# Attention over eight pairs of heads: five device loops, and the same passes written out

## The reference

```python
for blk in range(S // Q_BLOCK):
    q0 = blk * Q_BLOCK
    q1 = q0 + Q_BLOCK
    s = jnp.einsum("bhqd,bhkd->bhqk", q[:, :, q0:q1], k[:, :, :q1]).astype(jnp.float32)
    s = s + cum[:, :, q0:q1, None] - cum[:, :, None, :q1]
    causal = (q0 + jnp.arange(Q_BLOCK))[:, None] >= jnp.arange(q1)[None, :]
    p = jax.nn.softmax(jnp.where(causal, s, -jnp.inf), axis=-1)
    outs.append(jnp.einsum("bhqk,bhkd->bhqd", p.astype(v.dtype), v[:, :, :q1]))
```

## Time and profile before

| what | value |
| --- | --- |
| median of 3 runs | 2577.97 us |
| lowest and highest run | 2575.59 and 2579.7 us |
| the profiled execution | 2578.18 us |
| its span, first to last instruction | 2576.3 us |
| mean granted TensorE clock | 0.970 |
| PE busy in the span | 2410.6 us, 94% |
| DVE, ACT, POOL busy | 1350.7, 1160.1, 623.2 us |
| instructions executed | 41772 |
| instruction fetches, q8 and q14 | 59 packets, 0.97 MB, and 70 packets, 0.57 MB |

### The profile page before, as it was taken

How to read it: one execution, slowest core, us unless ns; L and a number is a source line. 1 busy time by engine, 2 the same in 40 slices (tenths; PEclk the granted TensorE clock), 3 DMA queues, 4 the chain that set the end, 5 groups by cost and what they waited for, 6 DMA issues and landing times. The chain is left out here.

```text
span 2576.3 us, 41772 instructions
## 1 busy us (share of the span) xinstructions
PE 2410.6 (94%) x13921; PEld 2081.1 (81%) x13921; DVE 1350.7 (52%) x2840; ACT 1160.1 (45%) x2136; POOL 623.2 (24%) x740
## 2 busy tenths in 40 slices
PE   8899999999996999999999999699689999993998
PEld 7688889998885888888888888587578888872786
DVE  4312121211007888888888888543245666575343
ACT  4211111111115888888888888510034555565100
POOL 0000000000002555455554555334300000000254
PEclk9899999999998999999999999899889999997999
DMA  5434343332116444544455444366344354343653
GB/s 183 113 113 126 113 130 114 124 106 78 65 49 148 98 98 111 128 113 98 96 124 129 99 98 96 106 215 212 125 154 123 123 156 138 117 146 120 246 189 138
DMA packets 216353, 325.75 MB, mean 126 GB/s; under 512 B 16672, under 2 KB 141664, under 8 KB 210016
## 3 DMA queue, kind: packets, MB, share of 16 engines
q1 hardware_dynamic: 215712, 323.68, 43.9%
q0 software_dynamic: 512, 0.53, 0.1%
HBM read 197.79 MB, written 126.35 MB: 126 GB/s over the span
## 5 line engine op out<-in xcount | busy, mean ns | idle before, releaser
L760 DVE TENSOR_TENSOR at_pl<-at_tps,at_ph 128x512 fp32r<-128x512 f32 (+3 forms) x640 | 370.5, 603 | 22.3 <-ACT at_ph L705 22.1
L705 ACT ACTIVATE at_ph<-at_tps 128x512 fp32r<-128x512 f32 (+3 forms) x640 | 313.0, 529 | 105.7 <-PE at_tps L627 98.9
L323 ACT ACTIVATE pa_stg<-pa_ps 128x512 fp32r<-128x512 f32 (+1 forms) x128 | 76.4, 599 | 608.4 <-PE pa_ps L227 608.3
L627 PE MATMUL at_tps<-at_ident,at_probs 128*128 128x128 f32 x2176 | 337.8, 273 | 1.5 <-DVE at_pl L760 1.2
L642 PE MATMUL at_ops<-at_ph,at_val 128*128 128x256 f32 (+1 forms) x1152 | 325.3, 304 | 2.3 <-DVE at_pl L760 2.1
L227 PE MATMUL pa_ps<-pa_xh,pa_wh 128*128 128x512 f32 x800 | 313.1, 391 | 12.1 <-DVE pa_stg L390 9.6
L695 ACT ACTIVATE at_probs<-at_probs,at_least 128x128 f32<-128x128 f32 (+15 forms) x256 | 307.7, 1202 | 19.0 <-DVE at_probs L751 18.9
L227 PE MATMUL pa_ps<-pa_xl,pa_wh 128*128 128x512 f32 x800 | 312.4, 390 | 0.0
L227 PE MATMUL pa_ps<-pa_xh,pa_wl 128*128 128x512 f32 x800 | 312.3, 390 | 0.0
L612 PE MATMUL at_sps<-at_k,at_q 128*128 128x512 f32 (+3 forms) x640 | 271.5, 424 | 26.4 <-DMA at_k<-forget_sums 22.0
L642 PE MATMUL at_ops<-at_pl,at_val 128*128 128x256 f32 (+1 forms) x1152 | 294.9, 281 | 0.0
(11 more groups left out here) (165 smaller groups left out, 4669.8 us busy)
## 6 DMA issues: line engine op xcount, KB each, us to landing
at_q<-q_halves SPq DMA_DIRECT2D x48, 512.0 KB
at_k<-k_halves SPq DMA_DIRECT2D x48, 512.0 KB
pa_wst<-in_attn_w_in SPq DMA_DIRECT2D x16, 1024.0 KB, 7.3
q_halves<-pa_stg SPq DMA_DIRECT2D x32, 512.0 KB, 3.7
k_halves<-pa_stg SPq DMA_DIRECT2D x32, 512.0 KB, 3.7
v_halves<-pa_stg SPq DMA_DIRECT2D x32, 512.0 KB, 2.8
at_val<-v_halves SPq DMA_DIRECT2D x16, 1024.0 KB, 16.9
y_gated<-rep_work SPq DMA_DIRECT2D x32, 512.0 KB, 2.9
```

The source lines that it names most:

```text
L323: nc.scalar.activation(out, source(kind, s), func, scale=scale).then_inc(evac_h, 1)
L627: mm = nc.tensor.transpose(tps[c % TB][:, k, :], probs[s % ROWS][:, t0:t0 + P], ident[:, :])
L705: nc.scalar.activation(ph[g % 2][:, j * PB:j * PB + n, i % 2 * P:(i % 2 + 1) * P], tps[c % TB][:, 0:n, :], ACT.Copy).then_inc(high_out, 1)
L760: nc.vector.tensor_tensor(pl[g % 2][at], tps[c % TB][:, 0:n, :], raw(ph[g % 2][at]), ALU.subtract)\
```

## The change

In each of the five blocks of `attend` the device loop becomes a Python loop over the same range. The body is then put down seven times (six on SP) with `it` as a plain number. The order of the work, all tiles and all waits stay.

```diff
@@ sync
             pair(0, False)
-            with sp.Fori(1, PAIRS - 1) as it:
+            for it in range(1, PAIRS - 1):
                 pair(it, False)
@@ gpsimd
             pair(0)
-            with pool.Fori(1, PAIRS) as it:
+            for it in range(1, PAIRS):
                 pair(it)
@@ tensor
-            with pe.Fori(1, PAIRS) as it:
+            for it in range(1, PAIRS):
                 for s in range(STEPS):
                     step(it, s, True)
@@ scalar
-            with act.Fori(1, PAIRS) as it:
+            for it in range(1, PAIRS):
                 for s in range(STEPS):
                     step(it, s, True)
@@ vector
-            with dve.Fori(1, PAIRS) as it:
+            for it in range(1, PAIRS):
                 for s in range(STEPS):
                     step(it, s, True)
```

## The result

The changed kernel takes 2580.94 us (median of 22 runs, 2577.55 to 2583.02), the kernel before in the same runs 2576.56 us (22 runs, 2572.98 to 2580.24). The ratio is 1.0016 with a 95% interval of 1.0009 to 1.0022: slower by 2 to 6 us. The ratio is just inside the 0.2% that the prediction called no change; the upper end of the interval is just outside. It had forecast 2579.1 us, with 2574.5 to 2584.0 as its range.

What follows compares the result with a forecast made beforehand. The prediction took PE to bound attention, with DVE not far behind. Its terms, -0.4 + 0 + 0 + 1.5 = +1.1 us on the profiled execution (2578.18 us, 0.2 above the median), gave 2579.1 us, range 2574.5 to 2584.

Steps and rivals of the forecast that it cites:

- 1. back edges: Attention's loop: six taken back edges go, which together cost PE 0.4 us; term -0.4 us.
- 2. register instructions: Attention's loop: register instructions go, at most 34 us on PE, but sequencers run ahead and hide them; term 0.
- 3. fetching PE's code: Attention: every pass of PE's code is now fetched, some 36 packets more; bounds 0 and 21.7 us, taken as 0.
- 4. the late L751: DVE in attention: pair 0's 0.36 us delay may recur in written-out pairs; bounds 0 and 3.1 us, term +1.5 us.
- more or less often than in half of the pairs: Sign on DVE in attention: term 4 is wrong if single late L751 come at such a rate.
- A: Rival: DVE's stall at attention's back edges counts in full, 18.6 us gained, giving 2559.6; chance 5%.
- B: Rival: register instructions were on PE's path in attention, 34 us gained, giving 2544; chance 2%.
- C: Rival: fetching PE's code stalls once in each pair, 21.7 us lost, giving 2600; chance 9%, smaller forms included.
- D's upper end: Case within the forecast (81% with D): DVE's odd 0.36 us comes in every attention pair, giving 2580.9.

Runs made afterwards that it cites:

- e2: The kernel before with DVE alone written out, the other engines keeping their loops: 846.4 us in attention, first to last L648.
- e1: The changed kernel with the loop put back on DVE alone: 841.8 us in attention, first to last L648.
- e3: The changed kernel with one more instruction on DVE ahead of attention: 842.4 us in attention, ratio 1.0009 to the kernel before.
- e4: The changed kernel with sixteen more instructions on DVE ahead of attention: 845.3 us in attention.
- e5: e3 with DVE's wait for PE's scores named before the wait for the transposes, so a row's first L751 carries the former: 840.0 us in attention.
- e9: e5 with, in later chunks, L751 carrying the wait for DVE's own minimum and the scores' wait alone: 836.0 us in attention; 2571.44 us, ratio 0.9983 to kernel before.
- e6: e5 with the same exchange of waits on ACT: 840.2 us in attention, ratio 0.9995 to the kernel before.
- e10: The kernel before, loops kept, with e9's order of waits on DVE: 842.6 us in attention, ratio 1.0002 to the kernel before.

## Why the prediction was right

The forecast, a little slower and hardly more than a measurement can tell, held, and its range held the median. As a difference it was too small: the measured 2 to 6 us lie wholly above its +1.1. It also owes something to luck, since two parts that it put at nothing, -1.0 and +2.2 us, partly cancel. Attention's 3.1 us come out of its terms like this:

| part | forecast | measured |
| --- | --- | --- |
| 1. back edges | -0.4 | -0.5: what the six passes of the kernel before, up to 106.04 us, have over 105.73 |
| 2. register instructions | 0 | -1.0: 7 x (105.73 - 105.59), the other engines' loops; -1.1 by e2 against the changed kernel; DVE's own 0 |
| 3. fetching PE's code | 0 | 0: e1 |
| 4. the late L751 | +1.5 | +2.5: 7 x 0.36, e3 and e4 |
| which wait stands alone | not seen | +2.2: 7 x (105.88 - 105.56), e3 against e5 |

The sum of what was measured is 2.5 + 2.2 - 0.5 - 1.0 = 3.2. Each part is from one profile, and the first is the least certain: DVE's six edges in e1 cost 1.3 us against e5 (634.7 us for the six passes, and 633.4).

Term 4 was the step with the wrong size. The prediction had found the event and its length in the earlier trace rows and left open what it was: "a packet of instructions ending there" or chance. It took half of the bound, since one of two fresh passes had it. The first was the cause as far as the count goes, and the event came in all seven pairs; by the prediction's own sign ("more or less often than in half of the pairs") the term is wrong. That attention's loss equals the upper bound of 3.1 us is partly chance, since terms 1 and 2 and the order of waits are in it too. What could have been done blind: to count DVE's instructions in the written order of the changed kernel up to that L751 and go on in steps of 128. That count gave seven exposed places in pairs 1 to 7 for this kernel, none for one instruction more and seven for sixteen more, before e3 and e4 ran.

Term 2 read "no gain" from pair 0's 77.87 us against 77.43. But pair 0 has the late L751 and the early wait carried, and under these two losses the gain can't be seen. e1 shows it: its pairs take 77.34 us for the same eleven groups. What the term also passed over is that register instructions carried waits. The prediction said that "waits on numbers remain in the instructions, or stand alone as before"; which of two waits stands alone changed, and this costs 0.09 us at each first L751 of a row where the scores come late.

The rivals. A, the whole DVE stall of 18.6 us: refuted, six edges on DVE are worth 1.3 us (e1 against e5, which both let L751 carry the late wait). B, 34 us of register instructions: refuted by e1 and e2, which leave about 1 us. C, PE's code late: refuted by e1 and by e9, whose pairs are all at 105.07 us with the whole code fetched. D's upper end is what happened. The stalls behind DVE's branches did go, and seven ends of a block came into the open. The Trainium skill, "Runtime: NRT & Kernel Launch", section "Instruction fetch mechanics", calls the crossing of a block mostly hidden, and on DVE the trace agrees for most of them: of 19 in pairs 1 to 7, twelve don't show.

What stays open: by its ratio the changed kernel loses 4.1 us and in attention 3.1. The other written-out kernels with 11 runs lean the same way: e3 has +2.3 us and in attention +0.2, e6 -1.3 and -2.0, e9 -4.4 and -6.2, while e10, with loops, has +0.5 and +0.4. This could be 1 to 2 us outside attention that go with longer code, but each interval is about 2 us wide on either side, and no stage of the profiles shows it.

## What to carry to other kernels

Before a loop is written out, compare a pass of it with the same work where it is already straight, and look at what differs: here that showed the late L751 before anything ran, while the 3 us stall behind a branch looked like the prize and was worth 0.2 us a pass. On an engine that hands work to the bounding one, look at which wait an instruction carries and which stands in front of it alone. Here it paid to let the first chunk's instruction carry the wait that was met last, and the later chunks' the wait for DVE's own result. A change that only moves code can be worth 0.1% (2.9 us in e3's attention), and one instruction of padding tells whether it did.

## What I had not expected of the hardware

- An L751 that stood exposed started 0.35 to 0.36 us late where a block of 128 of DVE's instructions ended, in straight code (all six late L751 with their waits met, at distances that are multiples of 128; none after a shift by one, six after a shift by sixteen; one packet of 8 KB on q14 for every 128 instructions in e2).
- A wait for PE's scores that stood alone on DVE cost 0.09 us more than the same wait carried by the instruction (0.12 us behind the semaphore against 0.02), and one for DVE's own result about 0.1 us (0.22 against 0.11 behind the read).
- PE's loop body of some 1,750 instructions was fetched once and then not at all; written out, it took 37 packets more on q8, at no cost that shows (e1).
